# Value projections of two attention layers: seven block products in place of eight, with 512 weight columns moving

## Chip, cores and metric

The kernel is one program on 1 core of a Trainium2 chip. The metric is its time on the device in microseconds (us), median of several runs. The profile is one further execution; times of rows are counted from its first instruction.

Engines: PE is the matmul engine (PEld its weight load), DVE, ACT and POOL work on vectors, SP issues DMAs. They run side by side, each its own instructions in order, and wait for each other on semaphores only. PE writes to PSUM (8 banks of 128 x 512 float32); all else is in SBUF.

## The reference

Two blocks of four sublayers each, on x of 512 tokens x 1024 features, in float32. The change bears on two projections `value = x @ W`, W of 1024 x 1024:

```python
# stick_breaking_mixer (layer 1 of the first block)
q, k, v = jnp.split(x @ w_qkv, 3, axis=-1)        # w_qkv 1024 x 3072
...                                               # 16 heads: scores, log_sigmoid, reverse cumsum, exp, weights @ v
# gla_mixer (layer 1 of the second block)
z = h @ w_in                                      # w_in 1024 x 3088
q, k, v, r, ga = jnp.split(z, [hk, 2 * hk, 2 * hk + hv, 2 * hk + 2 * hv], axis=-1)   # hk 512, hv 1024
log_a = jax.nn.log_sigmoid(ga @ w_a2 + b_a) / C_TAU   # ga has 16 columns; cumulated in chunks of 64 tokens
```

## The kernel before, in words

**Precision.** Each float32 operand is split into a rounded high part (`hi`, type fp32r) and the rest (`lo`), and a product is three matmuls: hi.hi, hi.lo, lo.hi. For weights ACT writes `w_hi` as a rounded copy of `w_stage` (`split`, L2088), DVE subtracts to get `w_lo` (`split`, L2970). Activations x are held as `x_hi`, `x_lo`, 8 chunks of 128 features x 512 tokens.

**Stages.** `plan_stages` lists the projections in order: ..., q, k, v (stick-breaking), w_o, ..., od_q, od_k, od_v (linear attention), od_r, od_out, .... A stage has iterations over 512 output columns; `wst`, `whi`, `wlo` are one buffer each of two halves of 128 x 2048. SP loads a half as soon as the `lo` part of the weights before it in that half is done; ACT and DVE split the next iteration's halves while PE works on this one's. In feature stages (q, k, od_q, od_k, od_r) the weights are stationary, 128 columns, and 512 tokens move; in the token stages v and od_v, the tokens are stationary (128) and 512 weight columns move: 2 iterations, 2 halves of the 1024 input features, 4 token tiles, 4 k, 3 matmuls (`token_stage` L1529, `token_products` L1513). DVE copies 8 results of 128 x 512 out (L3610, L3559).

**The gate stages** (gu0, gu1, conv0, conv1) already form most of their products from seven block products of halves (256 tokens, 512 inputs, 128 outputs), with 256 tokens moving (`seven_products`, L1371 on). For them DVE makes four sums of token blocks (L3042 to L3045, in the conv stages twelve steps from high and low parts, L3052 on), ACT rounds them (L2146) and DVE takes the low parts (L3074); sums of weight blocks are made by L3083, L3089, L3095, rounded by L2163 and lowered by L3101.

**Around v.** k is copied out by DVE (`copy_stage`, L3548), then eight tiny operations on gains (`gain_columns`, L3340). POOL waits for k's copies and swaps halves of q and k by DMA for each head (L829). While PE is in the last quarter of v, it does head 0's scores (`early`, `stick_scores(0)`, L1555 to L1565) and three more token tiles behind them. DVE then sets the sign bit (`stick_abs`, L3567), ACT does exp and log (L2427, L2433), DVE the softplus and sums of it (`stick_soft`, L3576 to L3591); the 16 heads follow one another in this loop.

**Around od_v.** PE does od_q, the low-rank gate (L1790), and od_k with four pairs of gate matmuls between its chunks (`gate_up`, L1801), into banks 4 to 7. ACT makes the log decay of it (`log_decay`, L2546: four bias activations L2550, Abs L2552, Exp L2554, Ln L2556), behind its two splits in od_k; DVE cumulates it (`cumulate`, L3796) in front of its work for od_v, and multiplies q and k by the decays (`decayed`, L3814) behind it.

**LayerNorm 1**, ahead of q, writes x_hi chunk by chunk on ACT (L2371) as DVE delivers; in norms 0 and 2 ACT also adds the bias to the residual behind each chunk (`finish`, L2365), in norm 1 it doesn't (L2373).

## Time and profile before

| what | value |
|---|---|
| time, median of 3 runs (lowest, highest) | 2387.3 us (2385.33, 2389.44) |
| the profiled execution's own time | 2386.84 us |
| its span, first to last instruction | 2385.0 us |
| mean granted clock of TensorE | 0.996 |
| busy share PE, DVE, ACT, POOL | 98%, 67%, 43%, 14% |
| stage v / stage od_v on PE begin at | 687.64 us / 1857.12 us |

The profile page gives busy times, the chain of work that ended last, and groups of instructions; the trace answers with timelines (start, duration, engine, line, operation, tile written <- tiles read, shape, count; in brackets the idle time before it and who ended it) and with windows (busy time of an engine in a stretch, and PEclk, the granted clock as a share of the full one). A PE duration is that of one matmul from start to end; several overlap, so the distance of starts is what one costs in a row.

### The profile page before, as it was taken

The numbers are of one execution on the slowest core, as the hardware profiler recorded it, in microseconds if no ns is written. First come the engines' busy times: TensorE is split into PE (matmuls) and PEld (weight loads), VectorE is DVE, ScalarE is ACT, GpSimd is POOL, SyncE is SP. The second block draws the span as 40 slices with busy tenths as digits, with TensorE's granted clock in tenths as the row PEclk, the third lists the DMA queues.
The fourth block names the chain that finished last, engine by engine and source line by source line (L and its number), as shares of the span: only waits on it lengthen the run. The fifth ranks groups of instructions, "written<-read, shape, count | busy, mean of one in ns | idle before, by whom it ended". The sixth has DMA issues, their size and how long they took to land.

```text
span 2385.0 us, 36878 instructions
## 1 busy us (share of the span) xinstructions
PE 2340.6 (98%) x14899; PEld 2037.7 (85%) x14899; DVE 1587.9 (67%) x2174; ACT 1029.4 (43%) x1352; POOL 339.0 (14%) x294
## 2 busy tenths in 40 slices
PE   7699999999999999999999999999999999999999
PEld 7688899988886678999878779999888877899987
DVE  8845877846536777777585546899534545799942
ACT  6421544532225725445234444556423344455622
POOL 6402000002002240000224241000121002000000
PEclk9899999999999999999999999999999999999999
DMA  2422333233232122332333313233332212333332
GB/s 58 104 97 90 105 107 105 83 101 113 89 99 69 40 94 85 107 103 82 96 107 110 89 64 114 82 105 89 101 102 85 93 66 71 89 107 107 85 107 85
DMA packets 328844, 219.67 MB, mean 92 GB/s; under 512 B 11188, under 2 KB 319050, under 8 KB 328618
## 3 DMA queue, kind: packets, MB, share of 16 engines
q1 hardware_dynamic: 322298, 208.46, 29.6%
q0 software_dynamic: 3024, 7.90, 1.4%
q8 instruction: 118, 1.93, 0.3%
q10 hardware_dynamic: 3360, 1.02, 0.2%
q14 instruction: 44, 0.36, 0.0%
HBM read 206.59 MB, written 2.10 MB: 87 GB/s over the span
## 4 chain that ended last, share of the span: by engine, by line
PE 90%; DVE 4%; POOL 3%; ACT 2%; issue 1%; SPq 0%; DMA 0%; DVEq 0%; ACTq 0%; POOLq 0%
PE psum L1380 9%; PE psum L1382 9%; PE psum L1381 9%; PE psum L1136 9%; PE psum L1138 9%; PE psum L1137 9%; PE psum L1349 3%; PE psum L1350 3%; PE psum L1351 3%; PE psum L1524 2%; PE psum L1525 2%; PE psum L1526 2%; PE psum L1248 1%; PE psum L1244 1%; PE psum L1245 1%; PE psum L1228 1%
## 5 line engine op out<-in xcount | busy, mean ns | idle before, releaser
L2093 ACT CAST w_hi<-w_stage 128x2048 fp32r<-128x2048 f32 x129 | 246.7, 1912 | 691.8 <-PE psum L1138 408.4
L2973 DVE TENSOR_TENSOR w_lo<-w_stage,w_hi 128x2048 fp32r<-128x2048 f32 x126 | 300.0, 2381 | 275.6 <-ACT w_hi L2093 275.6
L1380 PE MATMUL psum<-x_sum_hi,w_hi 128*128 128x256 f32 x1088 | 308.0, 283 | 0.2 <-issue 0.2
L1382 PE MATMUL psum<-x_sum_hi,w_lo 128*128 128x256 f32 x1088 | 307.9, 283 | 0.0
L1381 PE MATMUL psum<-x_sum_lo,w_hi 128*128 128x256 f32 x1088 | 307.9, 283 | 0.0
L2163 ACT CAST w_hi<-w_parts 128x1024 fp32r<-128x1024 f32 x204 | 213.3, 1049 | 200.9 <-PE psum L1382 111.1
L3101 DVE TENSOR_TENSOR w_lo<-w_parts,w_hi 128x1024 fp32r<-128x1024 f32 x204 | 248.1, 1219 | 51.7 <-ACT w_hi L2163 50.5
L1380 PE MATMUL psum<-x_hi,w_hi 128*128 128x256 f32 x816 | 230.9, 283 | 0.0
L1381 PE MATMUL psum<-x_lo,w_hi 128*128 128x256 f32 x816 | 230.9, 283 | 0.0
L1382 PE MATMUL psum<-x_hi,w_lo 128*128 128x256 f32 x816 | 230.9, 283 | 0.0
L1136 PE MATMUL psum<-hidden_raw_hi,w_hi 128*128 128x512 f32 x572 | 223.6, 391 | 0.3 <-DVE w_lo L2973 0.3
L1138 PE MATMUL psum<-hidden_raw_hi,w_lo 128*128 128x512 f32 x572 | 222.6, 389 | 0.0
L1137 PE MATMUL psum<-hidden_raw_lo,w_hi 128*128 128x512 f32 x572 | 222.6, 389 | 0.0
L1380 PEld LDWEIGHTS psum<-x_sum_hi,w_hi 128*128 128x128 f32 x1088 | 208.9, 192 | 1.0 <-issue 0.9
L1381 PEld LDWEIGHTS psum<-x_sum_lo,w_hi 128*128 128x128 f32 x1088 | 208.9, 192 | 0.1
L1382 PEld LDWEIGHTS psum<-x_sum_hi,w_lo 128*128 128x128 f32 x1088 | 208.9, 192 | 0.0
L1380 PEld LDWEIGHTS psum<-x_hi,w_hi 128*128 128x128 f32 x816 | 156.7, 192 | 0.0
L1381 PEld LDWEIGHTS psum<-x_lo,w_hi 128*128 128x128 f32 x816 | 156.7, 192 | 0.0
L1382 PEld LDWEIGHTS psum<-x_hi,w_lo 128*128 128x128 f32 x816 | 156.7, 192 | 0.0
L1136 PEld LDWEIGHTS psum<-hidden_raw_hi,w_hi 128*128 128x128 f32 x572 | 107.4, 188 | 23.2 <-issue 1.2
L1137 PEld LDWEIGHTS psum<-hidden_raw_lo,w_hi 128*128 128x128 f32 x572 | 107.4, 188 | 22.7 <-issue 0.5
L1138 PEld LDWEIGHTS psum<-hidden_raw_hi,w_lo 128*128 128x128 f32 x572 | 107.4, 188 | 22.3
(584 smaller groups left out, 5283.5 us busy)
## 6 DMA issues: line engine op xcount, KB each, us to landing
w_stage<-in_ffn_w_down_dram SPq DMA_DIRECT2D x64, 704.0 KB, 4.6
w_parts<-in_ffn_w_gu_dram SPq DMA_DIRECT2D x144, 256.0 KB, 3.4
w_parts<-in_ffn_w_gate_dram SPq DMA_DIRECT2D x64, 256.0 KB, 3.1
w_parts<-in_ffn_w_up_dram SPq DMA_DIRECT2D x64, 256.0 KB, 3.1
w_stage<-in_sb_w_qkv_dram SPq DMA_DIRECT2D x12, 1024.0 KB, 5.1
w_stage<-in_od_w_in_dram SPq DMA_DIRECT2D x12, 1024.0 KB, 5.2
w_stage<-in_ev_w_in_dram SPq DMA_DIRECT2D x10, 1024.0 KB, 5.0
w_stage<-in_ssm_w_glu_dram SPq DMA_DIRECT2D x8, 1024.0 KB, 5.5
```

What stands on the lines that cost most here:

```text
L1136: nc.tensor.matmul(dst, hi, x_hi, start=(start and k == 0), stop=False)
L1137: nc.tensor.matmul(dst, hi, x_lo, start=False, stop=False)
L1138: mm = nc.tensor.matmul(dst, lo, x_hi, start=False, stop=(stop and k == kn - 1))
L1349: nc.tensor.matmul(dst[u], hi, x_hi, start=(k == order[0]), stop=False)
L1350: nc.tensor.matmul(dst[u], hi, x_lo, start=False, stop=False)
L1380: nc.tensor.matmul(dst, hi, x_hi[:, k, :], start=(start and k == 0), stop=False, skip_group_check=True)
L1381: nc.tensor.matmul(dst, hi, x_lo[:, k, :], start=False, stop=False, skip_group_check=True)
L1382: mm = nc.tensor.matmul(dst, lo, x_hi[:, k, :], start=False, stop=(k == DC // 2 - 1), skip_group_check=True)
L2093: nc.scalar.copy(whi[:, half, :], wst[:, half, :]).then_inc(whi_done, 1)
L2163: nc.scalar.copy(ring_hi[:, slot:slot + 2, :], w_parts[tile][:, first:first + 2, :]).then_inc(rounded, 1)
L2973: V.tensor_tensor(wlo[:, half, :], wst[:, half, :], whi[:, half, :].bitcast(F32), ALU.subtract).then_inc(wlo_done, 1)
L3101: V.tensor_tensor(ring_lo[:, slot:slot + 2, :], w_parts[tile][:, parts, :], ring_hi[:, slot:slot + 2, :].bitcast(F32), ALU.subtract).then_ ...
```

## The change

v and od_v are made of seven block products as the gate stages are, but in the token form. x is cut in halves of tokens and of features (B11, B21, B12, B22: feature half first, token half second), W in halves of outputs and of inputs (A11, A12, A21, A22: output half first, input half second). One product takes 256 tokens (2 stationary tiles of 128), 512 inputs (4 k) and 512 weight columns: 2 x 4 x 3 = 24 matmuls. The order is S1, A11, S2, A12, S3, S4, A22; these names are those of the weight block (A) or the sum of weight blocks (S), each with its own token block or sum of token blocks (T1 to T4). Results are joined in PSUM banks 0 to 7 (W, Y, X, J of two banks each), with copies by ACT (`keep_z`, `fork`, `put`, `put_joined`) and sums by DVE (`token_seed`, `token_join`, `token_put`).

- Removed: token stages v and od_v; in each of them 4 splits of 128 x 2048 on ACT and on DVE, 4 loads of 1 MB and 8 copies out by DVE.
- SP: `token_loads`, two loads of 1 MB and four of 0.5 MB a stage, and the next stage's first two loads, each behind a wait of its own.
- DVE, v: 4 token sums of 128 x 1024 in stage k, behind its splits; then low parts of the sums, the sums of weight blocks (4 a stage, 128 x 2048) and the low parts of the seven (128 x 2048); two of k's copies stand behind the first of these. In od_q and od_k 12 steps (7 and 5) make the four token sums from the high and low parts. `cumulate` is cut in pieces and spread over od_v.
- ACT: 4 roundings of token sums (128 x 1024) and 7 of weight blocks (128 x 2048) a stage; in od_k `log_decay` comes first and `round_token_sums` behind it. `finish` now also runs in norm 1, since v's token sums read the residual.
- PE: 168 matmuls instead of 192 a stage. Head 0's scores come behind the first of the two tiles of A22; scores of head 1 wait for the last copy.

The core of the diff (indentation reduced; the layout of buffers, the counts of semaphores and the SP loads' addresses left out):

```diff
-("q", 2, 4, 4), ("k", 2, 4, 4), ("v", 2, 8, 4), ("w_o", 2, 4, 4), ("gu1", SEVEN["gu1"], 4, 2), ("down1", 8, 2, 1),
+("q", 2, 4, 4), ("k", 2, 4, 4), ("v", 0, 0, 0), ("w_o", 2, 4, 4), ("gu1", SEVEN["gu1"], 4, 2), ("down1", 8, 2, 1),
...
-("od_q", 1, 4, 4), ("od_k", 1, 4, 4), ("od_v", 2, 8, 4), ("od_r", 2, 4, 4), ("od_out", 2, 4, 4),
+("od_q", 1, 4, 4), ("od_k", 1, 4, 4), ("od_v", 0, 0, 0), ("od_r", 2, 4, 4), ("od_out", 2, 4, 4),
...
-return DC * (n > 0) + DC * (n > 2)
+return DC * min(n, 3)
...
+def token_loads(name):
...
+    last = ST[run[run.index(name) - 1]]
+    sp.wait_ge(part_done, last.part0)
+    if name == "od_v":
+        sp.wait_ge(ga_done, 1)
+    load(T_S3, 1, 0, whole, parts_landed[0])
+    load(T_A22, 1, 1, whole, parts_landed[0])
+    sp.wait_ge(wlo_done, ST[name].it0 * 2 - 1)
+    for ks in parts:
+        load(T_A11, 0, 0, ks, parts_landed[1])
+    for ks in parts:
+        load(T_A12, 0, 1, ks, a12_landed)
+    following = run[run.index(name) + 1]
+    sp.wait_ge(low_ready, token_low_count(name, T_S2 + 1))
+    sp.dma_start(tile_view(wst, following, 0), tile_source(following, 0, 0)).then_inc(w_landed[0], 16)
+    if name == "v":
+        sp.wait_ge(product_done, token_product_count(name, 2 * TOKEN_PRODUCTS))
+    else:
+        sp.wait_ge(low_ready, token_low_count(name, T_S4 + 1))
+    sp.dma_start(tile_view(wst, following, 1), tile_source(following, 0, 1)).then_inc(w_landed[1], 16)
...
+    def product(dst, n, tile, x, start=False):
+        (wh, wl), (xh, xl) = token_weights(name, n), x
+        rows = slice(tile * P, (tile + 1) * P)
+        for k in range(DC // 2):
+            hi, lo = xh[:, k, rows], xl[:, k, rows]
+            nc.tensor.matmul(dst[tile], hi, wh[:, k, :], start=(start and k == 0), stop=False, skip_group_check=True)
+            nc.tensor.matmul(dst[tile], hi, wl[:, k, :], start=False, stop=False, skip_group_check=True)
+            mm = nc.tensor.matmul(dst[tile], lo, wh[:, k, :], start=False, stop=(k == DC // 2 - 1), skip_group_check=True)
+        mm.then_inc(product_done, 1)
+    t1, t2, t3, t4 = ((token_sum_hi[name][n], token_sum_lo[name][n]) for n in range(4))
...
+    def arrived(n, x_sum=0):
+        pe.wait_ge(low_ready, token_low_count(name, n + 1))
+        if x_sum > 0:
+            pe.wait_ge(x_low, token_x_low_count(name, x_sum))
+    pe.wait_ge(evac_done, st.evac0 - 2)
+    arrived(T_S1, 1)
+    for tile in range(2):
+        product(token_w, T_S1, tile, t1, True)
+    if name == "od_v":
+        pe.wait_ge(la_link, GLA_HEADS)
+    arrived(T_A11)
+    for tile in range(2):
+        product(token_x, T_A11, tile, x_part(0, 0), True)
+    arrived(T_S2, 2)
+    for tile in range(2):
+        pe.wait_ge(copied, token_moved_count(name, 3 + tile))
+        product(token_x, T_S2, tile, t2)
+    arrived(T_A12)
+    for tile in range(2):
+        product(token_y, T_A12, tile, x_part(1, 0))
+    arrived(T_S3, 3)
+    for tile in range(2):
+        pe.wait_ge(added, token_moved_count(name, 1 + tile))
+        product(token_x, T_S3, tile, t3)
+    arrived(T_S4)
+    for tile in range(2):
+        product(token_w, T_S4, tile, x_part(1, 1))
+    arrived(T_A22, 4)
+    for tile in range(2):
+        pe.wait_ge(added, token_moved_count(name, 3 + tile))
+        product(token_x, T_A22, tile, t4)
+        if tile == 0 and early is not None:
+            early()
 def stick_scores(h):
     if h == 0:
-        pe.wait_ge(evac_done, ST["v"].evac1 - 4)
+        pe.wait_ge(evac_done, ST["v"].evac0 + 6)
     elif h == 1:
-        pe.wait_ge(evac_done, ST["v"].evac1 - 1)
+        pe.wait_ge(evac_done, ST["v"].evac1)
...
         nc.scalar.activation(xhi[:, c, tokens], res[:, c, tokens], ACT.Identity, bias=b[c]).then_inc(ln_hi, 1)
-        if n != 1 and c >= 2:
+        if c >= 2:
             finish(c - 2)
-    if n != 1:
-        finish(DC - 2)
-        finish(DC - 1)
+    finish(DC - 2)
...
+def round_token_sums(name):
+    for n, made in ((0, 1), (2, 2), (1, 3), (3, 4)) if name == "v" else ((2, 3), (3, 7), (0, 10), (1, 12)):
+        act.wait_ge(summed, token_summed_count(name, made))
+        nc.scalar.copy(token_sum_hi[name][n][:, :, :], token_sum[name][n][:, :, :]).then_inc(rounded, 1)
+def round_token_part(name, n):
+    last = ST[run[run.index(name) - 1]]
+    if n < 2:
+        act.wait_ge(part_done, last.part1 - 2 * (n == 0))
+    elif n < T_A22:
+        act.wait_ge(product_done, token_product_count(name, 2 * (n - 1)))
...
+def token_sums_and_first(name):
+    round_token_sums(name)
+    round_token_part(name, T_S1)
+    round_token_part(name, T_A11)
...
+def seven_token_stage(name, dst):
+    st = ST[name]
+    def keep_z(tile):
+        act.wait_ge(product_done, token_product_count(name, 2 * T_S1 + tile + 1))
+        nc.scalar.copy(token_z[name][:, tile, :], token_w[tile]).then_inc(copied, 1)
+    def fork(tile):
+        act.wait_ge(product_done, token_product_count(name, 2 * T_A11 + tile + 1))
+        act.wait_ge(evac_done, st.evac0)
+        nc.scalar.copy(token_y[tile], token_x[tile]).then_inc(copied, 1)
...
+    keep_z(0)
+    round_token_part(name, T_S2)
+    keep_z(1)
+    fork(0)
+    fork(1)
+    round_token_part(name, T_A12)
+    round_token_part(name, T_S3)
+    put(token_y, T_A12, 0, 0)
+    round_token_part(name, T_S4)
+    put(token_y, T_A12, 1, 0)
+    put_joined(0)
+    round_token_part(name, T_A22)
+    put_joined(1)
+    next_split(0, 2 * T_S3 + 2)
+    put(token_w, T_S4, 0, 1)
+    put(token_w, T_S4, 1, 1)
+    if name == "od_v":
+        next_split(1, 2 * T_S4 + 2)
 def stick_attention():
...
+        token_sums_and_first("v")
     elif name == "v":
...
         act.wait_ge(ga_done, 1)
         nc.scalar.copy(ga_t[:, :], bank[4]).then_inc(ga_copied, 1)
     elif name == "od_k":
-        split_stage(name)
         log_decay()
+        token_sums_and_first("od_v")
     elif name == "od_v":
-        split_stage(name)
+        seven_token_stage(name, gvt)
         decays()
     elif name == "ev_vb":
...
+def token_sums():
+    to = token_sum["v"]
+    first, second = slice(0, DC // 2), slice(DC // 2, DC)
+    dve.wait_ge(ln_a, affine_count(2))
+    b11, b12 = (res[:, first, tokens] for tokens in TOKEN_HALVES)
+    b21, b22 = (res[:, second, tokens] for tokens in TOKEN_HALVES)
+    token_step("v", 1, V.tensor_tensor(to[0][:, :, :], b11, b12, ALU.subtract))
+    token_step("v", 2, V.tensor_tensor(to[2][:, :, :], b22, b12, ALU.subtract))
+    token_step("v", 3, V.scalar_tensor_tensor(to[1][:, :, :], to[2][:, :, :], -1.0, b11, ALU.mult, ALU.subtract))
+    token_step("v", 4, V.scalar_tensor_tensor(to[3][:, :, :], to[1][:, :, :], -1.0, b21, ALU.mult, ALU.subtract))
...
+def token_sums_early():
...
+    b11, b21 = token_high_low(0, 0), token_high_low(1, 0)
+    token_difference(1, t3, token_high_low(1, 1), token_high_low(0, 1))
+    token_step("od_v", 4, V.tensor_tensor(t4, t3, b11[0], ALU.add))
+    token_step("od_v", 5, V.tensor_tensor(t4, t4, b11[1], ALU.add))
+    token_step("od_v", 6, V.tensor_tensor(t4, t4, b21[0], ALU.subtract))
+    token_step("od_v", 7, V.tensor_tensor(t4, t4, b21[1], ALU.subtract))
+def token_sums_late():
+    t1, t2, t3 = (token_sum["od_v"][n][:, :, :] for n in range(3))
+    b11 = token_high_low(0, 0)
+    token_difference(8, t1, b11, token_high_low(0, 1))
+    token_step("od_v", 11, V.scalar_tensor_tensor(t2, t3, -1.0, b11[0], ALU.mult, ALU.subtract))
+    token_step("od_v", 12, V.tensor_tensor(t2, t2, b11[1], ALU.subtract))
...
+def token_sum_lows(name):
+    for n, count in enumerate((1, 3, 2, 4) if name == "v" else (3, 4, 1, 2)):
+        dve.wait_ge(rounded, token_rounded_count(name, count))
+        V.tensor_tensor(token_sum_lo[name][n][:, :, :], token_sum[name][n][:, :, :],
+                        token_sum_hi[name][n][:, :, :].bitcast(F32), ALU.subtract).then_inc(x_low, 1)
...
+def token_first_parts(name):
+    dve.wait_ge(parts_landed[0], token_landed_count(name))
+    token_part_sum(name, 1, T_S1, T_S3, T_A22)
+    token_low(name, T_S1)
+    dve.wait_ge(parts_landed[1], token_landed_count(name))
+    token_part_sum(name, 2, T_S2, T_S1, T_A11)
+    token_part_sum(name, 3, T_S3, T_S3, T_A11)
+def token_second_parts(name):
+    token_low(name, T_S2)
+    dve.wait_ge(a12_landed, token_a12_count(name))
+    token_part_sum(name, 4, T_S4, T_S2, T_A12)
+    token_low(name, T_A12)
...
+def token_put(name, dst, tile):
+    dve.wait_ge(product_done, token_product_count(name, 2 * T_A22 + tile + 1))
+    dve.wait_ge(evac_done, ST[name].evac0 + 6 + tile)
+    V.tensor_scalar(dst[:, tile, 512:D], token_x[tile], -1.0, 0.0, ALU.mult, ALU.add).then_inc(evac_done, 1)
...
+def k_stage():
+    for half in range(2):
+        for u in range(2):
+            copy_unit("k", k_f, 1.0, 0, 2 * half + u)
+        split(ST["k"].it0 + 1, half)
+    token_sums()
+    for u in range(2):
+        copy_unit("k", k_f, 1.0, 1, u)
+    token_sum_lows("v")
+    token_first_parts("v")
+    for u in range(2):
+        copy_unit("k", k_f, 1.0, 1, 2 + u)
 def v_stage():
...
-    for i in range(st.iters):
-        last = i == st.iters - 1
-        split(i + st.it0 + 1, 0)
...
-            V.tensor_copy(v_t[:, n, i * 512:(i + 1) * 512], bank[4 * i + n]).then_inc(evac_done, 1)
-            if last and n == 0:
-                stick_abs(0)
-            if last and n == 1:
-                stick_soft(0)
-        if not last:
-            split(i + st.it0 + 1, 1)
+    token_low("v", T_A11)
+    token_second_parts("v")
+    for tile in range(2):
+        token_seed("v", tile)
+    token_low("v", T_S3)
+    token_low("v", T_S4)
+    for tile in range(2):
+        token_join("v", tile)
+    token_low("v", T_A22)
+    split(ST["v"].it0, 0)
+    token_put("v", v_t, 0)
+    stick_abs(0)
+    token_put("v", v_t, 1)
+    stick_soft(0)
...
+def od_q_stage():
+    for half in range(2):
+        for u in range(2):
+            copy_unit("od_q", gq, 128 ** -0.5, 0, 2 * half + u)
+        split(ST["od_k"].it0, half)
+    token_sums_early()
+def od_k_stage():
+    token_sums_late()
+    for u in range(2):
+        copy_unit("od_k", gk, 1.0, 0, u)
+    token_sum_lows("od_v")
+    token_first_parts("od_v")
+    for u in range(2):
+        copy_unit("od_k", gk, 1.0, 0, 2 + u)
+def od_v_stage():
+    token_low("od_v", T_A11)
+    cumulate_gates()
+    token_second_parts("od_v")
+    for tile in range(2):
+        token_seed("od_v", tile)
+    token_low("od_v", T_S3)
+    for h in range(2):
+        cumulate_head(h)
+    token_low("od_v", T_S4)
+    for tile in range(2):
+        token_join("od_v", tile)
+    token_low("od_v", T_A22)
+    split(ST["od_v"].it0, 0)
+    for h in range(2, GLA_HEADS):
+        cumulate_head(h)
+    token_put("od_v", gvt, 0)
+    cumulate_rest()
+    token_put("od_v", gvt, 1)
+    split(ST["od_v"].it0, 1)
 def decayed():
```

## Rows read from the trace of the kernel before

**Rows 1.** The page: engine busy, and the chain by engine

```profile
PE 2340.6 (98%) x14899; PEld 2037.7 (85%) x14899; DVE 1587.9 (67%) x2174; ACT 1029.4 (43%) x1352; POOL 339.0 (14%) x294
...
PE 90%; DVE 4%; POOL 3%; ACT 2%; issue 1%; SPq 0%; DMA 0%; DVEq 0%; ACTq 0%; POOLq 0%
```

**Rows 2.** Timeline of PE, 684 to 692: start us, us, line, op, operands

```profile
687.64 0.39 PE L1524 MATMUL psum<-w_hi,x_hi 128*128 128x512 f32 x1
```

**Rows 3.** Timeline of PE at the end of the stick-breaking value stage

```profile
723.00 0.39 PE L1555 MATMUL psum<-not_past,ident_rounded 128*128 128x512 f32 x1
...
724.84 0.50 PE L1524 MATMUL psum<-w_hi,x_hi 128*128 128x512 f32 x1
...
733.15 0.39 PE L1555 MATMUL psum<-not_past,ident_rounded 128*128 128x512 f32 x1
```

**Rows 4.** Timeline of PE around the linear attention's k stage

```profile
1843.70 1.12 PE L1801 MATMUL psum<-gate_low,gate_up 16*128 16x512 f32 x2
...
1857.12 0.39 PE L1524 MATMUL psum<-w_hi,x_hi 128*128 128x512 f32 x1
```

**Rows 5.** Timeline of DVE from stage k to the second head, 640 to 760

```profile
668.03 2.29 DVE L2973 TENSOR_TENSOR w_lo<-w_stage,w_hi 128x2048 fp32r<-128x2048 f32 x1 [1.13 <-ACT w_hi L2093]
676.40 1.38 DVE L3548 TENSOR_SCALAR k_feat<-psum 128x512 f32 x2 [6.08 <-PE psum L1351]
...
692.00 0.16 DVE L3343 TENSOR_TENSOR d_rows<-params 128x8 f32<-128x8 f32 x1
...
728.52 0.68 DVE L3576 SCALAR_TENSOR_TENSOR stick<-psum,stick 128x512 f32<-128x512 f32 x1
...
731.33 0.28 DVE L3591 TENSOR_TENSOR drop_sums<-stick,drop_sums 128x128 f32<-128x128 f32 x1
...
733.35 0.69 DVE L3610 COPY v_tok<-psum 128x512 f32<-128x512 f32 x1 [1.15 <-PE psum L1526]
734.66 1.55 DVE L3567 TENSOR_SCALAR stick<-psum 128x512 int32<-128x512 int32 x2 [0.62 <-PE psum L1561]
```

**Rows 6.** Timeline of ACT at the start of stage v, 640 to 760

```profile
687.84 1.91 ACT L2093 CAST w_hi<-w_stage 128x2048 fp32r<-128x2048 f32 x1 [8.96 <-PE psum L1138]
```

**Rows 7.** Timeline of DVE, first gate stage, 272 to 312

```profile
277.97 1.23 DVE L3045 SCALAR_TENSOR_TENSOR x_sum<-x_sum,residual 128x1024 f32<-128x1024 f32 x1
279.23 2.36 DVE L3083 TENSOR_TENSOR w_parts<-w_parts 128x1024 f32<-128x1024 f32 x2
281.51 4.62 DVE L3074 TENSOR_TENSOR x_sum_lo<-x_sum,x_sum_hi 128x1024 fp32r<-128x1024 f32 x4
```

**Rows 8.** Timeline of ACT, first gate stage, 272 to 312

```profile
281.29 1.99 ACT L2163 CAST w_hi<-w_parts 128x1024 fp32r<-128x1024 f32 x2
```

**Rows 9.** Timeline of ACT in norm 1, idle before in brackets

```profile
607.73 0.73 ACT L2371 ACTIVATE x_hi<-residual,params 128x512 fp32r<-128x512 f32 x1 [1.32 <-DVE residual L3512]
```

**Rows 10.** Timeline of DVE, linear attention, 1795 to 1925

```profile
1827.28 2.29 DVE L2973 TENSOR_TENSOR w_lo<-w_stage,w_hi 128x2048 fp32r<-128x2048 f32 x1 [1.35 <-ACT w_hi L2093]
1845.75 1.38 DVE L3548 TENSOR_SCALAR gla_k<-psum 128x512 f32<-128x512 f32 x2 [16.18 <-PE psum L1351]
```

**Rows 11.** Timeline of ACT, linear attention, 1795 to 1925

```profile
1859.19 2.42 ACT L2550 ACTIVATE gla_log_a<-psum,params 128x512 f32<-128x512 f32 x4
...
1865.54 2.01 ACT L2556 ACTIVATE gla_exp<-gla_exp,one_col 128x2048 f32<-128x2048 f32 x1
```

**Rows 12.** Timeline of PE in the state-space stage, 60 to 100

```profile
76.42 0.63 PE L1035 MATMUL psum<-d_rows,ident 128*16 128x64 f32 x16 [9.56 <-POOL cl_im_neg L753]
...
80.78 0.65 PE L1044 MATMUL psum<-cl_im_neg,b_cols 64*16 64x128 f32 x8
...
81.59 0.39 PE L1044 MATMUL psum<-cl_im_neg,b_cols 64*16 64x128 f32 x8
...
89.35 0.51 PE L1088 MATMUL psum<-cl_re,states 64*64 64x128 f32 x8 [2.85 <-DVE marks L2953]
```

**Rows 13.** Windows of PE: us, busy (instructions), PEclk, DMA share, GB/s

```profile
64.50:65.00 0.50, 0.26 (x3) 0.50 0.68 107
```

More of the change, by code:

```diff
@@ L64 @@
 TOKEN_HALVES = (slice(0, HALF), slice(HALF, SEQ))
-TOKEN_STAGES = ("v", "ev_v", "ev_vb", "od_v")
+TOKEN_STAGES = ("ev_v", "ev_vb")
 HALVED_LAST = {"ev_out": 2, "cdown0": 1, "od_out": 2}
@@ L75 @@
 RING = 8
+TOKEN_STEPS = {"v": 4, "od_v": 12}
+TOKEN_PRODUCTS = 7
 HIDDEN_ORDER = (0, 2, 3, 4, 5, 6, 9, 7, 8, 1, 10, 11, 12, 13, 14, 15, 16, 17, 18, 19, 20, 21)
@@ L506, in before, with tokens_before, sevens_before, iters_before @@
             return sum(SEVEN_ITERS[other] for other in list(SEVEN)[:list(SEVEN).index(name)])
+        def tokens_before(name):
+            return [other for other in TOKEN_STEPS if run.index(other) < run.index(name)]
+        def sevens_before(name):
+            return [other for other in SEVEN if run.index(other) < run.index(name)]
+        def iters_before(name):
+            return sum(SEVEN_ITERS[other] for other in sevens_before(name))
         def products_count(name, i, n):
-            return (before(name) + i) * PRODUCTS + n
+            return (before(name) + i) * PRODUCTS + 14 * len(tokens_before(name)) + n
@@ L524, in summed_count @@
         def summed_count(name, i, n):
             steps = sum(X_STEPS[other] for other in list(SEVEN)[:list(SEVEN).index(name) + 1])
+            steps += sum(TOKEN_STEPS[other] + 4 for other in tokens_before(name))
             return steps + (before(name) + i) * 6 + n
         def copied_count(name, i, n):
-            return (before(name) + i) * 4 + n
+            return (before(name) + i) * 4 + 4 * len(tokens_before(name)) + n
         def added_count(name, i, n):
-            return (before(name) + i) * 4 + n
+            return (before(name) + i) * 4 + 4 * len(tokens_before(name)) + n
@@ L537, in gated_count, with token_summed_count, token_moved_count @@
+        def token_summed_count(name, n):
+            steps = sum(X_STEPS[other] for other in sevens_before(name)) + iters_before(name) * 6
+            return steps + sum(TOKEN_STEPS[other] + 4 for other in tokens_before(name)) + n
+        def token_moved_count(name, n):
+            return iters_before(name) * 4 + 4 * len(tokens_before(name)) + n
         def gated_count(name, i, n):
@@ L592, in tile_source @@
                 w = {"ssm_out": "ssm_w_out", "w_o": "sb_w_o", "ev_out": "ev_w_out_2", "od_out": "od_w_out_2"}[name]
-                return wcols(t[w][0], i * 512 + half * 256)
+                return wcols(t[w][0], i * 512 + (half * 256 + first * 512))
             if name in ("gu0", "gu1"):
@@ L610, in tile_source @@
                 return rows[:, :, bass.ds(i * 512 + col, 512)]
-            return wcols(t[w][0], i * 512 + half * 256 + col)
+            return wcols(t[w][0], i * 512 + (half * 256 + first * 512 + col))
         def tile_view(w, name, half):
@@ L1527, in token_products, with token_stage @@
                 return mm
[L1529 removed]
+            def token_stage(name, xh, xl):
                 st = ST[name]
[L1532 to L1543 removed]
+                for half in range(2):
+                    pe.wait_ge(wlo_done, st.it0 * 2 + half + 1)
+                    for n in range(TT):
+                        token_products(bank[4 + n], name, half, n, xh, xl).then_inc(part_done, 1)
@@ new lines, in token_sums_and_first, with put, put_joined, next_split @@
+            def token_sums_and_first(name):
[3 more added lines that the diff above has]
+            def seven_token_stage(name, dst):
+                st = ST[name]
+                def keep_z(tile):
[5 more added lines that the diff above has]
+                    nc.scalar.copy(token_y[tile], token_x[tile]).then_inc(copied, 1)
+                def put(from_, n, tile, half):
+                    act.wait_ge(product_done, token_product_count(name, 2 * n + tile + 1))
+                    nc.scalar.copy(dst[:, 2 * half + tile, 0:512], from_[tile]).then_inc(evac_done, 1)
+                def put_joined(tile):
+                    act.wait_ge(added, token_moved_count(name, 3 + tile))
+                    nc.scalar.activation(dst[:, 2 + tile, 512:D], token_j[tile], ACT.Copy, scale=-1.0).then_inc(evac_done, 1)
+                def next_split(half, done):
+                    act.wait_ge(w_landed[half], st.it0 * 16 + 16)
+                    act.wait_ge(product_done, token_product_count(name, done))
+                    nc.scalar.copy(whi[:, half, :], wst[:, half, :]).then_inc(whi_done, 1)
+                keep_z(0)
[16 more added lines that the diff above has]
+                    next_split(1, 2 * T_S4 + 2)
@@ L3812, in cumulate @@
                                 ALU.subtract).then_inc(cum_done, 1)
+            def od_q_stage():
+                for half in range(2):
+                    for u in range(2):
[30 more added lines that the diff above has]
+                split(ST["od_v"].it0, 1)
             def decayed():
```

163 lines of the change are left out of this document (115 added, 48 removed).

## The prediction, made before the changed kernel was run

> **What bounds the kernel now.** I read the page first: PE is busy for 98% of the span and carries 90% of the chain that ended last [rows 1]. So a matmul taken out of a dense stretch is worth its slot, and a wait put in front of PE costs its full length. Next I read PE's timeline where the stick-breaking value stage begins. The reader should look at starts there, not at the 0.39 us that one matmul lasts: the stage starts at 687.64 and its 157th instruction, the first score of head 0, at 723.00 [rows 2, 3], so 156 matmuls took 35.36 us, **0.2267 us each**. The linear attention's value stage starts at 1857.12 [rows 4], with 192 matmuls of the same form. Last I read DVE and ACT ahead of both stages, because the change gives them work that must be done before PE gets there.
>
> **Matmuls.** Before: 4 token tiles x 8 k x 2 column halves x 3 = 192. Seven products of 2 tiles x 4 k x 3 are 168. Form and width stay, so the slot stays: 24 x 0.2267 = 5.44 us less per stage, **-10.88 us**. By the isolated spacing that the Trainium skill states (TensorE: Matmul & The Clock Gate, "Back-to-back issue gap": columns over 2.4 GHz plus some 2.5 ns, 0.216 us) it would be -10.4 us; the trace has 0.2267. One product, 24 slots, is also 5.44 us.
>
> **Prices of the new vector work.** A block or sum of blocks of *weights* is 4 k x 512 = 128x2048 in this form, twice the gate stages' pieces. Its sum or low part on DVE costs 2.29 us [rows 5], its rounding on ACT 1.91 [rows 6]. A *token* sum is 128x1024: 1.26 us a step in a dependent row, four low parts 4.6 us [rows 7], a rounding 1.05 [rows 8].
>
> **Norm before q: nothing.** ACT gets 8 activations of 0.73 us, one behind each chunk's rounding, where it idles 1.32 us waiting for DVE [rows 9]. With that cover gone it would be at most 5.8 us.
>
> **Stick-breaking, the first product.** DVE ends k's last split at 670.3 [rows 5]; four token sums end at 675.4; the two k copies stay at 676.40 to 677.7 [rows 5]; four low parts to 682.3; first weight sum to 684.5; ACT rounds it to 686.5; its low part is there at 688.8. PE wants it at 687.64 and **waits 1.2 us**.
>
> **The second product.** Between this low part and that of A11, DVE has in its queue: two weight sums (4.6 us), two k copies that stood earlier before (1.35), the eight gain operations (0.2 us apart, first at 692.00 before [rows 5]: 1.55), then the low part itself, 2.29. That is 9.8 us, done at 698.6. PE has one product, 5.44 us, to bridge it: from 688.8 to 694.3. It **waits 4.3 us**. All others can be hidden: from here a rounding waits only for the slot that PE freed, 0.2 us after a product's end, 1.9 us for it and 2.3 for the low part are 4.4, inside 5.44, with 0.5 to 1.0 us in hand; the sums of results (below 0.8 us each, by the copies' 0.69 [rows 5]) and ACT's copies stand beside them. Only where a PSUM copy of ACT stands ahead of a rounding (A12) the hand is 0.5 us. Loads are no limit: SP issues the first two when q is done, 43 us ahead, the rest when k's first-half weights are split, over 20 us ahead; the next stage's two loads queue behind S2's low part and the last product, also long before use.
>
> **The end of it.** The last product's first tile ends at 698.6 + 5 x 5.44 + 2.72 = 728.5, then 1.84 us of head 0's scores (723.00 to 724.84 before [rows 3]), then 12 matmuls: 733.1, the same as the 733.15 of before [rows 3]. The two waits have eaten this stage's 5.44 us. But behind the scores there were 36 matmuls and now are 12, and what is late next is DVE: scores of head 1 now wait for the last copy (0.2 us behind the end, 0.69 long), and head 0's softplus, 728.52 to 731.61 before [rows 5], stands *behind* that copy: 733.9 to 737.0. Head 1's magnitudes, which set the pace of all heads, start at 737.0 and not at 734.66 [rows 5]: **+2.3 us**.
>
> **Linear attention, the first product.** DVE has room for its twelve steps: od_k's second split ends at 1829.6 [rows 10], 12 x 1.26 end at 1844.7, the copies keep 1845.75, where DVE had idled 16.18 us [rows 10]. The place to look is ACT: the log decay now stands *ahead* of the token sums' roundings. The last gate pair starts at 1843.70 and lasts 1.12 [rows 4], the last bias is added at 1845.5; absolute value, exponential, logarithm: 1859.19 to 1867.55 before, less four bias steps of 2.42, 5.9 us [rows 11]. ACT is free at 1851.4. DVE waits for the third rounding (1854.3), then four low parts (1858.9), the weight sum (1861.2), its rounding (1863.2), its low part (1865.5). PE wants it at 1857.12: it **waits 8.4 us**. Bounds: 7.5 (no hand-overs) and 9.5 (1 us more for them).
>
> **Its second product.** The same queue without the gain operations: 4.6 + 1.3 + 2.3 = 8.1 us against 5.44, **2.6 us**. The log decay's prefix sums, cut in pieces, stand in later gaps; the tightest is S2's low part, 0.3 us ahead of PE. The splits for od_r and the decayed products are ready by my schedule 6 us before PE wants them.
>
> **The clock.** It may fall in the waits. The trace has: a gap of 2.85 us (before 89.35) that left it up; 0.50 of full, 1.2 of 2.4 GHz, at 64.5 us, among small transposes with waits and before the idle 9.56 us that end at 76.42; and from 76.42 dense work that is still slow at 80.78 (0.65 us a group) and fast at 81.59 (0.39) [rows 12, 13]. Five microseconds at half speed lose about **2.4 us**. After 8.4 us I expect it down; but there PE bridges to the second product, and 5.44 + 2.4 us just fill the 8.1 us: the loss takes the place of the 2.6 us wait, no more. After 4.3 us, nearer to 2.85 than to 9.56, I take it as held: 0, with 2.4 as the other end. The Trainium skill (TensorE: Matmul & The Clock Gate, "Why this matters for your kernels") tells to keep PE free of longer idle gaps in mid-kernel, as the clock goes back to half; this speaks against the change, and by it the 2.4 us are due: rival (a).
>
> **Sum.** -10.88 + 1.2 + 4.3 + 2.3 + 8.4 + 2.6 = **+7.9 us** on the profiled execution, 2386.84 us (span 2385.0 and 1.84 around it), 0.46 under the median of 2387.3. Against the median: **2395.2 us**.
>
> **Rivals.**
> (a) *The clock falls in the 4.3 us wait of the stick-breaking stage*, nothing absorbs it there since PE bounds all that follows: 2397.6 us. For it the fall at 64.5, against it the gap of 2.85.
> (b) *Not slower: the linear attention's first wait is short.* Place: ACT's queue in od_k. If the roundings weren't held by the log decay, DVE's low parts would follow the copies at 1847.1 and the first low part be there at 1858.3: a wait of 1.2 instead of 8.4, sum +0.7, 2388.0 us. It decides from a wait under 5.3 us (sum under +4.8). Against: ACT works in order, and the code has the decay first.
> (c) *Faster: the low parts of first and second products come on time in both stages*, because sums or low parts overlap or take under 1.3 us: -10.88 + 2.3, 2378.7 us. Against: the split's 2.29 us for this very shape.
> (d) *Worse:* hands of 0.3 to 1.0 us are used up (A12, S2, both stages) by longer hand-overs, some 1 us at each of five products: 2400 us.
> That it doesn't do what it says, a wider slot with sums as stationary operand, has nothing for it: the gate stages use such sums.
>
> **Chances.** Forecast 0.42, (a) 0.27, (b) 0.11, (c) 0.06, (d) 0.10, between forecast and (b) 0.04. No change means within 0.2%, 4.8 us, about what a measurement of this kernel can tell. (b) lies within it, (c) is faster, the others slower. With the stall's bounds the range goes from 2390.5 to 2400: it takes in forecast, (a), and the better half of (d).
>
> **What would show it.** In stage v PE idles about 1.2 us before its first product and 4.3 us before the second, both ended by DVE's low part; head 1's magnitudes start 3.9 us behind the last matmul, 1.5 before. At the start of od_v PE idles over 7 us, with ACT's logarithm directly before the roundings, and the granted clock is 0.50 for some us behind it. From product three on there are no gaps over 0.3 us. Waits under half of these, or a first wait under 5.3 us in od_v, would make the prediction wrong.

## The result, and the profile after

| | before | changed | ratio (95%) |
|---|---|---|---|
| median, us | 2387.7 (2385.3 to 2389.4, 6 runs) | 2398.3 (2395.8 to 2402.6, 6 runs) | 1.0047 (1.0035 to 1.0060) |
| profiled execution, us | 2386.8 | 2400.7 | |
| its span, us, and granted clock | 2385.0, 0.996 | 2398.9, 0.991 | |

The change costs **10.6 us** on the medians. Predicted were 7.9, and a range that ends at 2400.0. The direction and the range held; the size was under by 2.7.

The page of the changed kernel, its busy times and its chain by engine, beside [rows 1]:

```profile
PE 2339.6 (98%) x14851; PEld 2035.0 (85%) x14851; DVE 1644.1 (69%) x2208; ACT 1064.9 (44%) x1394; POOL 338.7 (14%) x294
...
PE 88%; DVE 6%; POOL 3%; ACT 2%; issue 1%; SPq 0%; DMA 0%; DVEq 0%; ACTq 0%; POOLq 0%
```

48 matmuls are gone (14899 to 14851), yet PE's busy time fell by 1.0 us only, where 48 slots of 0.2267 are 10.9. The span grew, and the chain now runs over DVE for 6% and not 4. So look for two things: waits, and matmuls that became longer. The waits of PE with what ended them, changed kernel, 680 to 760 us:

```profile
PE psum L1659 <- DVE w_lo L3851: 3.8, 1, 3.8
PE psum L1717 <- ACT stick L2595: 1.7, 2, 1.0
PE psum L1659 <- issue: 1.1, 1, 1.1
PE psum L1711 <- ACT stick L2595: 1.1, 1, 1.1
PE psum L1711 <- DVE v_tok L3884: 0.9, 1, 0.9
```

and 1850 to 1917 us:

```profile
PE psum L1659 <- issue: 8.4, 1, 8.4
PE psum L1659 <- DVE w_lo L3851: 0.2, 1, 0.2
```

L1659 is the first matmul of the new products. "issue" stands where the first product starts: the engine waits for low part and token-sum low part together, and the view finds no single releaser. Timeline of PE at these places (start, us, line, operands, idle before):

```profile
691.25 0.47 PE L1659 MATMUL psum<-w_hi,v_sum_hi 128*128 128x512 f32 x1 [1.08 <-issue]
...
700.72 0.50 PE L1659 MATMUL psum<-w_hi,x_hi 128*128 128x512 f32 x1 [3.78 <-DVE w_lo L3851]
...
701.83 0.63 PE L1659 MATMUL psum<-w_hi,x_hi 128*128 128x512 f32 x1
702.25 0.63 PE L1660 MATMUL psum<-w_lo,x_hi 128*128 128x512 f32 x1
...
704.70 0.39 PE L1660 MATMUL psum<-w_lo,x_hi 128*128 128x512 f32 x1
...
1874.01 0.77 PE L1659 MATMUL psum<-w_hi,od_v_sum_hi 128*128 128x512 f32 x1 [8.38 <-issue]
...
1882.10 0.47 PE L1659 MATMUL psum<-w_hi,x_hi 128*128 128x512 f32 x1 [0.17 <-DVE w_lo L3851]
```

Behind the 3.78 us wait the starts are 0.43 us apart and no longer 0.23: the clock. Windows of the changed kernel (us, PE busy (instructions), PEld, DVE, ACT, POOL, then **PEclk**, DMA share, GB/s):

```profile
700.70:705.10 4.40, 4.38 (x12) 3.49 (x13) 4.37 (x2) 0.00 (x0) 0.97 (x2) 0.61 0.46 113
744.00:745.50 1.50, 0.50 (x1) 0.19 (x1) 0.61 (x2) 1.50 (x3) 1.26 (x1) 1.00 1.11 314
745.50:752.30 6.80, 6.54 (x23) 4.67 (x24) 4.08 (x9) 3.71 (x6) 2.05 (x4) 0.50 0.21 46
752.30:760.00 7.70, 7.03 (x52) 5.11 (x50) 4.41 (x9) 4.45 (x7) 2.34 (x4) 1.00 0.15 34
1865.60:1874.00 8.40, 0.03 (x1) 0.02 (x1) 6.31 (x5) 3.70 (x2) 0.00 (x0) 0.67 0.00 0
1874.00:1878.80 4.80, 4.79 (x12) 3.79 (x12) 4.73 (x3) 0.00 (x0) 0.00 (x0) 0.51 0.00 0
```

Behind 640 us it fell three times (0.50 is the level of 1.2 GHz, 1.00 that of 2.4): in v's second product, among heads 1 and 2 of the attention (745.5 to 752.3), and inside the long wait of od_v, where it stayed down for most of the first product. The kernel before had 1.00 from 82 us to its end.

**Where the time went.** The same PE instruction is found in both traces, and its start compared. Columns: how much later than in the first profile of before everything is when the work of stage k begins ("ahead"), what stage v and the attention add (640 to 850 us of before), the stretch between (850 to 1843.70 [rows 4]), and od_v (1843.70 to the first matmul of od_r, 1900.99). The experiments' profiles stand in the same table:

| kernel | ahead | v and attention | between | od_v | median, us |
|---|---|---|---|---|---|
| changed | +2.4 | +6.4 | -0.4 | +5.5 | 2398.3 |
| changed, again (e8) | +1.2 | +5.9 | -0.3 | +5.5 | 2399.1, one run |
| e1 roundings first | +2.2 | +3.6 | -0.4 | +1.2 | 2393.6 |
| e2 v filled | +4.9 | +3.3 | -0.4 | +5.5 | 2396.6 |
| e3 od_v filled | 0.0 | +6.4 | -0.4 | +7.1 | 2398.1 |
| e4 v's low part early | -0.8 | -1.8 | -0.4 | +5.5 | 2391.6 |
| e5 head 1 early | +0.8 | -3.0 | -0.4 | +5.5 | 2389.8 |
| e6 all orders | +2.2 | -4.3 | -0.3 | -5.2 | **2377.7** |
| before, again (e7) | +5.1 | 0.0 | 0.0 | 0.0 | 2391.8, one run |

"Ahead" isn't the change: it arises in the first 100 us, where the two profiles of before alone differ by 5.1 us (waits for DMA, POOL and the clock). Without it the profiled pair differs by 6.4 - 0.4 + 5.5 = 11.5 us, which fits the 10.6 of the medians (each row of the table is one execution, and that of the changed kernel was 2.4 us over its median). Nothing is lost or won in the norm ahead of q: the shift is 2.36 us at 270 and at 640.

### The profile page after: what moved, and what is told of

Its sections match the earlier page's. It is cut to its first block, busy times and chain, and to the rows that moved or that the text cites. A ratio compares the mean times of both kernels' runs of the same rounds, so it can differ in the third digit from the quotient of the medians.

```text
span 2398.9 us, 36783 instructions
## 1 busy us (share of the span) xinstructions
PE 2339.6 (98%) x14851; PEld 2035.0 (85%) x14851; DVE 1644.1 (69%) x2208; ACT 1064.9 (44%) x1394; POOL 338.7 (14%) x294
## 3 DMA queue, kind: packets, MB, share of 16 engines
q10 hardware_dynamic: 3360, 1.02, 0.2%
## 4 chain that ended last, share of the span: by engine, by line
PE 88%; DVE 6%; POOL 3%; ACT 2%; issue 1%; SPq 0%; DMA 0%; DVEq 0%; ACTq 0%; POOLq 0%
PE psum L1488 9%; PE psum L1490 9%; PE psum L1489 9%; PE psum L1244 9%; PE psum L1246 9%; PE psum L1245 9%; PE psum L1457 3%; PE psum L1458 3%; PE psum L1459 3%; PE psum L1356 1%; PE psum L1352 1%; PE psum L1353 1%; PE psum L1659 1%; PE psum L1661 1%; PE psum L1660 1%; PE psum L1336 1%
## 5 line engine op out<-in xcount | busy, mean ns | idle before, releaser
L2249 ACT CAST w_hi<-w_stage 128x2048 fp32r<-128x2048 f32 x118 | 225.6, 1912 | 593.9 <-PE psum L1246 390.5
L3203 DVE TENSOR_TENSOR w_lo<-w_stage,w_hi 128x2048 fp32r<-128x2048 f32 x118 | 281.7, 2387 | 244.7 <-ACT w_hi L2249 244.6
```

The costliest lines, as they stand in the source:

```text
L2249: nc.scalar.copy(whi[:, half, :], wst[:, half, :]).then_inc(whi_done, 1)
L3203: V.tensor_tensor(wlo[:, half, :], wst[:, half, :], whi[:, half, :].bitcast(F32), ALU.subtract).then_inc(wlo_done, 1)
```

## The experiments

All medians but those of e7 and e8 are of 5 to 11 runs, beside 22 runs of before at 2388.2 (e1 to e4) and 15 at 2387.8 (e5 to e8). "Under the changed kernel" compares with its 2398.3, beside which before had 2387.7; so such differences are good to some tenths only, and the ratios are the firmer numbers.

**e1, ACT's order in od_k.**

```diff
+                round_token_sums("od_v")
                 act.wait_ge(la_link, GLA_HEADS)
                 nc.scalar.activation(ge[:, :, :], la[:, :, :], ACT.Abs).then_inc(la_link, 1)
...
     log_decay()
-    token_sums_and_first("od_v")
+    round_token_part("od_v", T_S1)
+    round_token_part("od_v", T_A11)
```

> ACT's four roundings of the token sums stand behind the last bias addition of the log decay and ahead of its absolute value, exponential and logarithm; nothing else moves. Theory (the log decay's 5.9 us on ACT held the roundings): roundings 1853.9 to 1857.8, sum S1 on DVE at 1862.4, log decay until 1863.7, S1's low part at 1868.0, so PE's first wait in od_v is 2.4 us and no longer 8.4, the clock stays at 1.00, and the second wait, which the slow product had filled, comes back with about 2.7 us. Net -5.7 us against the changed kernel. Rival (the roundings wait for DVE's sums or for the token-sum low parts, not for the log decay): the first wait stays above 7 us, 0 us net. If the clock falls all the same in one of the two waits left, -4 us.

2393.6 us, ratio 1.0023 (1.0014 to 1.0032), 4.6 under the changed kernel; od_v 4.3 us shorter. PE in e1:

```profile
1865.12 0.47 PE L1659 MATMUL psum<-w_hi,od_v_sum_hi 128*128 128x512 f32 x1 [2.45 <-issue]
...
1873.21 0.47 PE L1659 MATMUL psum<-w_hi,x_hi 128*128 128x512 f32 x1 [2.39 <-DVE w_lo L3853]
```

and its window behind the second wait:

```profile
1873.50:1877.00 3.50, 3.50 (x11) 2.78 (x10) 3.45 (x4) 0.00 (x0) 0.00 (x0) 0.60 0.00 0
```

The first wait went from 8.38 to 2.45 (expected 2.4): the log decay's place on ACT had held it. The second came back, 2.39, and the clock fell behind it, hence 4.3 and not 5.7. Its attention shows +3.6 where the changed kernel has +6.4, though nothing in it differs: here the clock stayed up among the heads.

**e3, the same wait at full clock.**

```diff
     pe.wait_ge(evac_done, st.evac0 - 2)
+    if name == "od_v":
+        for m in range(36):
+            nc.tensor.matmul(token_w[0], xhi[:, m % 4, 0:P], xhi[:, m % 4, :], start=True,
+                             stop=True, skip_group_check=True)
     arrived(T_S1, 1)
```

> 36 matmuls of 512 columns whose result is thrown away stand on PE ahead of od_v's first product, 36 x 0.227 = 8.2 us, about the length of its first wait. Nothing the product waits for moves. It prices the clock alone. Theory, as in the prediction (the clock's loss only takes the place of the second wait): granted clock 1.00, the first product 5.4 instead of 7.9 us, and a second wait of 2.6 us where the changed kernel has 0.2; net 0, within 1 us. Rival (the loss is paid): net -2.3 us. Second rival (the 2.6 us wait makes the clock fall behind it): +1.5 us.

2398.1 us, ratio 1.0038 (1.0024 to 1.0052): 0.1 from the changed kernel, net 0 as in the theory. PE in e3, and its window:

```profile
1871.73 0.50 PE L1659 MATMUL psum<-w_hi,od_v_sum_hi 128*128 128x512 f32 x1 [0.19 <-DVE w_lo L3855]
...
1879.87 0.77 PE L1659 MATMUL psum<-w_hi,x_hi 128*128 128x512 f32 x1 [2.40 <-DVE w_lo L3855]
```

```profile
1880.00:1883.50 3.50, 3.50 (x9) 2.79 (x10) 3.45 (x4) 0.00 (x0) 0.00 (x0) 0.54 0.00 0
```

Compare the distance from the first product to the second: 1879.87 - 1871.73 = 8.14 us at full clock with a wait of 2.40; 1882.10 - 1874.01 = 8.09 in the changed kernel at half clock with a wait of 0.17. **DVE's queue sets it, and the half clock behind the long wait costs nothing.** In this profile the clock then fell behind the 2.40 us wait, where nothing absorbs it, and od_v was 1.6 longer (the second rival). But this was the slowest of its five runs, 2400.1 us at a granted clock of 0.992; the others are at 0.994 and 0.995, and the median run is one of them. Whether the clock fell there in those is not known.

The runs that leave od_v as it is say the same: in e2, e4 and e5 the first wait is 8.38 us too, the clock rises sooner than in the changed kernel, the second wait is 0.85, 0.83 and 0.74 us, and the second product starts 8.10, 8.10 and 8.09 us behind the first.

**e2, the wait in v at full clock.**

```diff
+    if name == "v":
+        for m in range(17):
+            nc.tensor.matmul(token_x[0], xhi[:, m % 4, 0:P], xhi[:, m % 4, :], start=True,
+                             stop=True, skip_group_check=True)
     arrived(T_A11)
```

> 17 matmuls of 512 columns whose result is thrown away stand on PE between the first and the second product of stage v, 17 x 0.227 = 3.9 us, the length of the second wait. The second product starts where it did. It prices the clock that fell behind this wait, 3.4 us at half, and asks what made the clock fall a second time among heads 1 and 2, 6.8 us at half. Theory A (each fall has its own cause, the second one the waits around the late head 1): -1.7 us against the changed kernel, the fall among the heads stays. Theory B (the second fall comes of the first): both go, -1.7 - 2.5 = -4.2 us.

2396.6 us, ratio 1.0031 (1.0019 to 1.0043), 1.7 under the changed kernel by medians that are each uncertain by more than 1. The profile is the slowest of its six runs, 2400.2 us, with 4.9 of "ahead" in it. Windows of e2:

```profile
690.00:745.00 55.00, 52.13 (x241) 41.25 (x239) 38.36 (x39) 26.58 (x28) 5.52 (x9) 1.00 0.23 69
745.00:750.00 5.00, 3.85 (x17) 2.78 (x18) 2.92 (x7) 2.23 (x4) 1.54 (x2) 0.69 0.32 87
```

The clock is 1.00 through all of stage v, and falls among the heads all the same, for a shorter time (0.69 over 5 us); the -3.1 us of the table against the changed kernel are this shorter fall and the 1.7 us of the first one. Theory A: that fall has its own cause, it isn't an echo of the first.

**e4, DVE's order in v.**

```diff
     token_part_sum(name, 2, T_S2, T_S1, T_A11)
+    if name in A11_EARLY:
+        token_low(name, T_A11)
     token_part_sum(name, 3, T_S3, T_S3, T_A11)
...
-    token_low("v", T_A11)
     token_second_parts("v")
+    gain_columns()
...
     k_stage()
-    gain_columns()
```

Here `A11_EARLY` is ("v",).

> DVE's order in stage v alone: A11's low part stands between the sums S2 and S3, ahead of S3, the last two copies of k and the gain columns, and the gain columns stand behind A12's low part. Theory (the 9.8 us queue of DVE ahead of A11's low part is the second wait): the low part is there at 695.7, PE's second wait of 3.8 us goes, and with it the fall of the clock behind it (1.7 us): -5.5 us against the changed kernel. No later product gets a wait over 0.3 us. Rival (what holds it is ACT's rounding of A11 or the load): the wait stays over 2 us. If the fall among heads 1 and 2 goes too: -8.0 us.

2391.6 us, ratio 1.0018 (1.0009 to 1.0027), 6.7 under the changed kernel. PE in e4 at the start of the second product, and a window from stage v to head 3:

```profile
693.39 0.39 PE L1662 MATMUL psum<-w_hi,v_sum_lo 128*128 128x512 f32 x1
693.61 0.39 PE L1660 MATMUL psum<-w_hi,x_hi 128*128 128x512 f32 x1
```

```profile
687.00:750.00 63.00, 57.94 (x300) 45.15 (x300) 47.15 (x59) 35.12 (x40) 11.46 (x16) 1.00 0.26 76
```

No wait and full clock. The stage with its attention is at -1.8 us, which is -5.44 + 1.25 (first wait) + 2.3 (head 1) = -1.9. So the queue on DVE was the second wait, and all of v's loss is now in two terms. Against the changed kernel's profile that is 8.2 us less, near the 8.0 expected if the fall among the heads goes too, which it did; by the medians it is 6.7.

**e5, the seam to the attention.** On top of e4:

```diff
     stick_abs(0)
-    token_put("v", v_t, 1)
-    stick_soft(0)
+    stick_soft(0, lambda: token_put("v", v_t, 1), lambda: stick_abs(1))
```

`stick_soft` calls the first behind its first half and the second ahead of its three small sums.

> The kernel with A11's low part early in stage v (e4), and in it DVE's order at the seam to the attention: the last copy of v stands between the two halves of head 0's softplus, and head 1's magnitudes ahead of head 0's three small sums. Theory (head 0's softplus behind the last copy is what makes head 1 late): head 1's magnitudes start 2.0 us behind the last matmul of the stage, 3.6 in e4, and the whole attention moves by that: from the start of stage v to the dense stages behind the attention -1.6 us against e4, which stood at -1.85 us against the kernel before. Rival (PE's scores of head 1 or ACT set the pace): less than 0.5 us. PE's wait ahead of head 2's scores, 1.05 us in the changed kernel, should nearly go.

2389.8 us, ratio 1.0007 (0.9998 to 1.0016), which can't be told from before; in the table 1.2 us under e4 (-3.0 against -1.8), where 1.6 were expected. DVE in e5:

```profile
729.58 0.43 DVE L3909 CAST soft_hi<-stick 128x512 fp32r<-128x512 f32 x1
730.09 0.69 DVE L3887 TENSOR_SCALAR v_tok<-psum 128x512 f32<-128x512 f32 x1
730.70 0.95 DVE L3903 SCALAR_TENSOR_TENSOR stick<-psum,stick 128x768 f32<-128x768 f32 x1
732.52 1.56 DVE L3894 TENSOR_SCALAR stick<-psum 128x512 int32<-128x512 int32 x2 [0.87 <-PE psum L1718]
```

Head 1's magnitudes (732.52) now wait 0.87 us for PE's scores, and these for the last copy of v: the softplus was in the way for 1.2 us, and behind it the copy, the scores and DVE form a chain of their own. 2.6 us behind the last matmul (729.67, and 0.23 for it), 3.8 in the changed kernel, 1.5 before.

**e6, all orders at once.** e1, e4 (in od_v too) and e5, S1's rounding ahead of the absolute value, and, in `token_first_parts`, the low parts of the token sums behind the sum S1:

```diff
     token_part_sum(name, 1, T_S1, T_S3, T_A22)
+    token_sum_lows(name)
     token_low(name, T_S1)
...
-    token_sum_lows("v")
     token_first_parts("v")
...
-    token_sum_lows("od_v")
     token_first_parts("od_v")
```

> All orders at once, in both stages: sum S1 ahead of the token sums' low parts; A11's low part between sums S2 and S3; gain columns, and the log decay's first steps on DVE, behind A12's low part; token-sum roundings and S1's rounding ahead of the log decay's absolute value; the seam of e5. Theory (all of the loss is order on DVE and ACT and none is in the matmuls): no wait over 0.3 us on PE in either stage, the clock at 1.00 through both; stage v with its attention -1.85 - 1.08 - 1.6 = -4.5 us against the kernel before, od_v -5.4 us, -0.4 us that all changed kernels show behind the attention: -10.3 us, 2377.9 us against 2388.2. Rival (the seven-product form has costs of its own, such as lows on DVE that take turns with each other): each stage keeps a wait of 1 us or more, and the sum ends at -7 us or less.

**2377.7 us, ratio to before 0.9957 (0.9943 to 0.9970)**: 10.1 us faster than before, 20.6 than the changed kernel, 0.2 from what was expected. The waits of PE in e6 over stage v and the attention, 680 to 760 us:

```profile
PE psum L1718 <- ACT stick L2596: 2.0, 2, 1.0
PE psum L1712 <- DVE v_tok L3890: 0.9, 1, 0.9
```

over od_v, 1850 to 1905 us:

```profile
PE psum L1660 <- DVE w_lo L3854: 0.3, 1, 0.3
```

and the clock from stage k to the end:

```profile
640.00:2370.00 1730.00, 1721.68 (x10407) 1488.70 (x10406) 1203.45 (x1524) 795.03 (x1062) 225.18 (x196) 1.00 0.31 92
```

od_v gained 5.2 us with a wait of 0.3 left: that is the 5.44 of 24 matmuls, and the seven-product form costs PE nothing of its own there. In v 1.1 of the 5.44 us are still lost (-4.3 in the table): head 1 is late as in e5, behind the 0.9 us wait for the last copy.

**e7 and e8, both kernels once more**, unedited, for the clock.

> The kernel before once more, for the places where its clock falls. If the fall among heads 1 and 2 belongs to the change, the clock stays at 1.00 from 82 us to the end here, as in the first profile, and the wait of 2.8 us ahead of the state products at 89 us is passed at full clock or not, which shows how far such a wait decides.

> The changed kernel once more. Behind the 3.8 us wait of stage v and the 8.4 us wait of od_v the clock falls again, at the same place and by 3.4 and 10.2 us. The fall among heads 1 and 2 comes or not: of four profiles with the same waits there so far (0.9, 1.1 and 1.0 us) three had it and one did not, at 2.8 us more for the attention with it.

Before, again:

```profile
88.00:92.00 4.00, 1.90 (x24) 1.50 (x18) 3.79 (x8) 0.00 (x0) 3.99 (x8) 0.55 0.72 96
...
640.00:2380.00 1740.00, 1732.59 (x10457) 1497.87 (x10456) 1149.68 (x1491) 764.14 (x1029) 224.93 (x196) 1.00 0.31 91
```

Changed, again, windows and the starts of od_v's first two products:

```profile
698.00:699.00 1.00, 0.00 (x0) 0.00 (x0) 1.00 (x1) 0.18 (x1) 0.00 (x0) 0.64 0.59 131
...
700.00:705.00 5.00, 5.00 (x13) 3.84 (x13) 3.88 (x2) 0.00 (x0) 0.50 (x1) 0.50 0.65 195
...
745.00:752.00 7.00, 6.46 (x29) 4.70 (x29) 4.85 (x9) 4.07 (x7) 2.61 (x4) 0.76 0.21 46
```

```profile
1872.37 0.77 PE L1659 MATMUL psum<-w_hi,od_v_sum_hi 128*128 128x512 f32 x1 [8.40 <-issue]
...
1880.46 0.47 PE L1659 MATMUL psum<-w_hi,x_hi 128*128 128x512 f32 x1 [0.75 <-DVE w_lo L3851]
```

Before, no fall behind 640 us, as in its first profile. The wait ahead of the state products is 3.05 us here, but the clock had fallen before it began (0.50 from 88.5 us on), so this run does not tell what such a wait decides. Changed, all three again, but not of the lengths expected. In v the clock was down from inside the wait (it ended at 699.53) to 705; among the heads it was down for less time; and in od_v it rose sooner, so that the wait ahead of the second product is 0.75 and not 0.17. The distance from first to second product is 8.09 us again: however long PE is slow there, DVE's queue decides.

## Why the prediction was right, and where it was short

The measured terms for stage v come from the changed kernel's first profile, with its 2.36 us "ahead" taken off.

| step | predicted | measured | shown by |
|---|---|---|---|
| 48 matmuls | -10.88 | -5.4 in od_v | e6: -5.2 with a 0.3 us wait |
| norm ahead of q | 0 | 0.0 | shift 2.36 at 270 and at 640 |
| v, first product | +1.2 | +1.25 (691.25 for 690.00) | e4, e6 |
| v, second product | +4.3 | +4.0 (700.72 - 691.25 - 5.44) | e4: gone |
| clock behind it | 0 | +1.7 | e2, e4: 1.00 |
| head 1 | +2.3 | +2.3 | e4: what is left; e5: 1.2 of it is the softplus |
| clock among the heads | not seen | +2.6, in 4 profiles of 6 with these waits | e2; e1 and e4 without |
| od_v, first product | +8.4 | +8.55 | e1: 2.45 |
| od_v, second, or the clock in its place | +2.6 | +2.65 (8.09 - 5.44) | e3: 8.14 at full clock; e8: 8.09 |
| behind the attention | none | -0.4 | all changed kernels; cause open |

**The mechanism held at every wait.** Each of the four was where the steps put it and within 0.3 us by the starts in the table. The view names DVE's low part for the second wait of each stage; for the first ones it names none, but there too the low part ends just before PE starts (in v it runs from 688.86 to 691.15, PE starts at 691.25). The four roundings ahead of it in od_v took 3.88 us on ACT; the 1854.3 of the prediction has 0.97 for each and not the 1.05 that it had stated, a slip that did no harm. The working by queue (what stands ahead of the low part on DVE, what stands ahead of the rounding on ACT) is what made this possible, and e1 and e4 show both queues by moving single entries. Rival (b), a short first wait in od_v, fell with the 8.38 us; (c) with all of them; of (d) there is nothing: no wait over 0.3 us from product three on, in either stage.

**The step that failed is "After 4.3 us, nearer to 2.85 than to 9.56, I take it as held: 0".** The clock fell, as rival (a) says, at 1.7 us and not 2.4: the eleven steps from 700.72 to 704.93 take 4.21 us where 2.49 were due. With this wait the clock fell in all four profiles that have it (changed, e1, e3, e8). The Trainium skill's advice (TensorE: Matmul & The Clock Gate, "Why this matters for your kernels") was right to weigh against the change here. The fault was in the evidence: one passage of one trace was read as a bound. The wait of 2.85 us [rows 12] that "left it up" stands in the changed kernel's trace too, as 2.73 us, and there the clock fell:

```profile
90.58 0.71 PE L1196 MATMUL psum<-cl_re,states 64*64 64x128 f32 x8 [2.73 <-DVE marks L3183]
```

```profile
90.50:93.50 3.00, 2.92 (x56) 2.92 (x60) 2.90 (x5) 0.00 (x0) 2.98 (x5) 0.50 0.77 132
```

The other profiles have this place too. Waits of 2.78 us (e3), 2.82 (e4) and 3.24 (e5) left the clock up, with waits of 2.83 (e1), 3.69 (e8) and 4.07 (e6) it was down at their end or with the first matmuls behind them. Here are e5 and e1, each with the wait and a window behind it. The longer wait left the clock up and the shorter one didn't, so the prediction's "nearer to 2.85 than to 9.56" had no footing in one passage:

```profile
90.02 0.51 PE L1197 MATMUL psum<-cl_re,states 64*64 64x128 f32 x8 [3.24 <-DVE marks L3184]
90.00:92.00 2.00, 1.98 (x64) 1.90 (x64) 1.93 (x3) 0.00 (x0) 1.98 (x4) 1.00 0.76 144
...
89.77 0.71 PE L1196 MATMUL psum<-cl_re,states 64*64 64x128 f32 x8 [2.83 <-DVE marks L3185]
90.00:92.00 2.00, 2.00 (x44) 2.00 (x44) 1.93 (x3) 0.00 (x0) 1.98 (x4) 0.50 0.80 144
```

**And the clock was priced only at the long waits.** The prediction ended its account at head 1's magnitudes (+3.9 by the table's terms, and 740.87 - 734.66 - 2.36 = 3.85 measured). But a late head 1 made ACT late with head 0's weights, so PE waited 0.88, 1.05 and 1.02 us within 9 us, where a head of before has only the last, and behind them the clock read 0.50 for 6.8 us, 2.6 us of time. It isn't a sure cost. With these three waits it fell in the profiles of the changed kernel, e2, e3 and e8, not in e1 and e4. Without the 1.05 one (e5, e6) it stayed up both times, and so it did in both of before. That this wait decides is not shown by so few; it stays open. The trace of before had a hint that short waits can be enough: the fall that the prediction cites at 64.5 us came behind waits of 1.04 and 0.26 us only.

```profile
62.85 0.70 PE L989 MATMUL psum<-ident,x_natural 64*128 64x64 f32 x8 [1.04 <-ACT x_feat L2024]
63.82 0.71 PE L989 MATMUL psum<-ident,x_natural 64*128 64x64 f32 x8 [0.26 <-ACT x_feat L2024]
64.00:64.50 0.50, 0.50 (x8) 0.39 (x7) 0.50 (x1) 0.50 (x1) 0.50 (x2) 0.97 0.67 98
```

With 1.7 for the first fall the sum would have been +9.6, 2396.9 us; with the second fall, where it comes, +12.2, 2399.5. The median of 2398.3 lies between and is nearer to rival (a)'s 2397.6 than to the forecast. That it stayed inside the range is in part luck: the room above (a) was left for the better half of (d), of which nothing came, and a loss that nobody had foreseen took it.

## What to carry to other kernels

When PE is dense and a change takes matmuls out at a stage's head, write down the queue ahead of the first two operands on every engine that prepares them; the gain is there only if each preparation is done before its product. Here 10.1 of the 10.9 us of matmuls came back by reordering, without removing an instruction. Put an early operand's low part ahead of sums that are needed a product later, and small roundings ahead of a long elementwise chain. Price each new PE wait twice, by its length and by a spell at half clock behind it, unless PE afterwards waits for another engine anyway: then the second price is free.
